# Hybrid pool/HGRN2/RWKV-7 decoder on one core: block-by-block layers against layer 1 first and layer 2 as one pipeline over 32 units

## What is computed

```python
# layer 0 ("layer 1" in this text)
u = h @ ev_w_in                                   # 1024 -> 6 x 512
y_pool = causal_pool_mixer(u[..., :o1], pool_w, pool_scale)      # windows 2, 4, 8, 16
y_hgrn = hgrn2_mixer(u[..., o1:o2], u[..., o2:o3], u[..., o3:o4], lb, hgrn_onorm_g)
out = (concat(y_pool, y_hgrn) * silu(u[..., o4:])) @ ev_w_out
# layer 1 ("layer 2" in this text)
xx = token_shift(h) - h
xm = h[None] + xx[None] * mu[:, None, None, :]    # six mixes: r k v z w a
r, k, v, z = xm[:4] @ w_rkvz
decay = exp(-exp(-softplus(-(w0 + tanh(xm[4] @ w1) @ w2)) - 0.5))
a = sigmoid(a0 + (xm[5] @ a1) @ a2)
# per head of 64, per token: state = state*decay + (state @ -kk) (kk*a)^T + v k^T ; y = state @ r
y = group_norm(y) + bonus
out = (y * silu(z)) @ rw_w_out
```

## Time and profile before

| | us |
|---|---|
| median of 3 runs | 3750.0 (3747.28 to 3751.33) |
| the profiled execution's own time | 3747.55 |
| its span, first to last instruction | 3745.8 |
| PE busy | 3389.4 (90%) |
| DVE busy | 1645.2 (44%) |
| ACT busy | 1264.9 (34%) |
| mean granted TensorE clock | 0.944 of full |

### The profile page before, as it was taken

One profiled execution on the slowest core, in us unless ns is written; L12 is line 12 of the kernel. 1 busy time (PEld: TensorE's weight loads), 2 busy tenths in 40 slices (PEclk: granted clock), 3 DMA queues, 4 the chain that ended last, 5 costly groups with the idle time before them and its releaser, 6 DMA issues.

```text
span 3745.8 us, 76696 instructions
## 1 busy us (share of the span) xinstructions
PE 3389.4 (90%) x33546; PEld 2031.9 (54%) x33546; DVE 1645.2 (44%) x3445; ACT 1264.9 (34%) x2356; POOL 278.4 (7%) x383
## 2 busy tenths in 40 slices
PE   2898799999899869999989887999998987999998
PEld 1554356666356436666646544666654653566663
DVE  7354544443235463444325445444422455444442
ACT  0343233333333323333324332343333333233332
POOL 0010100000011010000000101000000101000000
PEclk8999799999999979999999987999999998899999
DMA  7221211110321121101031211011112211110201
GB/s 315 69 69 68 69 30 43 48 48 30 108 63 55 49 69 48 45 28 48 30 125 46 103 46 47 25 48 48 47 60 83 69 69 46 47 48 25 65 30 51
DMA packets 269508, 230.46 MB, mean 62 GB/s; under 512 B 15548, under 2 KB 251256, under 8 KB 266104
## 3 DMA queue, kind: packets, MB, share of 16 engines
q1 hardware_dynamic: 266872, 217.18, 17.8%
q0 software_dynamic: 2304, 8.39, 0.6%
HBM read 208.76 MB, written 16.78 MB: 60 GB/s over the span
## 4 chain that ended last, share of the span: by engine, by line
PE 81%; DVE 11%; ACT 4%; issue 2%; DMA 1%; SPq 0%; DVEq 0%; ACTq 0%; another core or an unknown queue 0%
PE bank L550 20%; PE bank L424 14%; PE bank L517 8%; PE bank L500 5%; PE bank L649 4%; PE bank L636 4%; PE bank L645 3%; PE bank L457 3%; PE bank L421 3%; DVE xm L1357 2%; PE bank L561 2%; DVE arena L1440 2%; DMA xm<-in_ada_w 1%; PE bank L401 1%; PE bank L692 1%
## 5 line engine op out<-in xcount | busy, mean ns | idle before, releaser
L550 PE MATMUL bank<-xm,wring 128*128 128x512 f32 x2048 | 946.2, 607 | 33.8 <-DVE xm L1357 26.6
L550 PEld LDWEIGHTS bank<-xm,wring 128*128 128x128 f32 x2048 | 381.6, 193 | 504.8 <-issue 445.2
L424 PE MATMUL bank<-arena,wring 128*128 128x512 f32 x1280 | 580.1, 593 | 14.0 <-ACT xm L823 10.2
L424 PEld LDWEIGHTS bank<-arena,wring 128*128 128x128 f32 x1280 | 230.7, 190 | 259.1 <-issue 254.4
L517 PE MATMUL bank<-wring,yT 128*128 128x512 f32 x608 | 281.6, 627 | 30.5 <-DVE yT L1501 20.4
L986 ACT COPY arena<-bank 128x256 f32<-128x256 f32 x256 | 96.6, 377 | 489.1 <-PE bank L649 489.1
L1482 DVE COPY arena<-bank 128x64 f32<-128x64 f32 x256 | 57.6, 225 | 402.4 <-PE bank L682 398.4
L517 PEld LDWEIGHTS bank<-wring,yT 128*128 128x128 f32 x608 | 121.5, 201 | 190.5 <-issue 153.4
L1614 POOL COPY r_Q<-ident 128x512 f32<-128x512 f32 x160 | 98.2, 613 | 1634.5 <-PE bank L649 1626.7
L500 PE MATMUL bank<-wring,yT 128*128 128x512 f32 x416 | 216.4, 626 | 0.0
L649 PE MATMUL bank<-arena,r_Q 64*64 64x32 f32 x5120 | 206.9, 224 | 0.0
(11 more groups left out here) (270 smaller groups left out, 5204.1 us busy)
## 6 DMA issues: line engine op xcount, KB each, us to landing
wring<-in_rw_w_rkvz SPq DMA_DIRECT2D x128, 512.0 KB, 6.3
wring<-in_ev_w_in SPq DMA_DIRECT2D x96, 512.0 KB, 5.2
xm<-in_ada_w SPq DMA_DIRECT2D x16, 1536.0 KB, 11.8
wring<-in_ev_w_out SPq DMA_DIRECT2D x32, 512.0 KB, 7.9
wring<-in_rw_w_out SPq DMA_DIRECT2D x32, 512.0 KB, 4.4
xm<-in_x POOLq DMA_DIRECT2D x16, 512.0 KB, 5.3
arena<-in_x SPq DMA_DIRECT2D x16, 512.0 KB, 5.1
residual_scratch<-arena SPq DMA_DIRECT2D x4, 2048.0 KB, 7.5
```

The lines of the kernel that those rows point to most:

```text
L424: mm = pe.matmul(pj[:, :], w[:, k, :], hT[:, k, 1:1 + TB], start=(k == 0), stop=(k == KC - 1))
L550: mm = pe.matmul(bank[1 if m == PROJ_Z else 0][:, :], w[:, k, :], xmv[MIX_OF[m]][:, k, :], start=(k == 0), stop=(k == KC - 1))
```

## The change

Layer 1 is done for all four blocks first. Each block's input of layer 2 (`h1T`, normed and turned, with one column of the block before) is saved to a DRAM buffer `h1_mem`, its rows to `resid`, tile by tile. The norm of the next block's layer 1 stands inside the output projection of layer 1 (before its last tile group); the layer-2 norm of the block before stands after the first group's projections. The norms scale their rows in place, so a tile is stored before it is scaled.

Layer 2 then runs as one pipeline over 32 units v = 8 b + p. Its input is loaded into slots 4 to 7 of the weight ring (`h_in`), so slots 0 to 3 hold one weight tile each for K, R, V, Z. The mixes of the next block are made inside the periods, in two steps per slice: ACT multiplies by (1 - mu), DVE adds mu times the shifted input: W and A in unit 5 of a block, K, R and V in unit 6, Z in unit 7; `lora_down` ends unit 5's period. The output projection of the block before stands in unit 1, in one piece and without an early part; its residual takes the old rows through one buffer `r_x1`. Only the last block keeps `out_early`.

```diff
@@ sizes and slots
-ARENA = 17184
+ARENA = 19760
-LORA_SLOT = 7
+NB = SEQ // TB
+NU = NB * RP
+LORA_SLOT = 0
+OUT1_ORDER = [2, 0, 1, 3, 4, 5, 6, 7]
+    for v in range(NU):
...
+        for i, m in enumerate("krvz"):
+            uses[i].append((m, v))
+        for i, last in ((0, 2), (1, 2), (2, 1), (3, 1)):
+            if b and p == last:
+                uses[i].append(("o", b - 1))
...
+    for i in range(4, 8):
+        uses[i] += [("h", 0), ("h", 1), ("o", 0), ("h", 2), ("o", 1), ("h", 3), ("o", 2), ("o", 3)]
@@ sync: layer 1
+            group_weights(0, 0)
             for b in range(n_blocks):
+                group_weights(b, 1)
+                if b:
+                    save_input(b - 1)
+                    sp.wait_ge(S["n_tr"], (norm_at(b - 1, 1) + 1) * KC)
                 for j in range(JT):
                     sp.dma_start(xres[:, j, :], x_v[b:b + 1][0][:, j, :]).then_inc(x_in[j], 16)
+                group_weights(b, 2)
+                group_weights(b, 3)
                 for s in range(SLOTS):
+                    load(s, ("o0", b), w_out_v[0][s])
+                if b + 1 < n_blocks:
+                    group_weights(b + 1, 0)
+                for j in range(JT):
+                    sp.wait_ge(S["ob"], b * 8 + 2 * (j + 1))
+                    sp.dma_start(resid[b:b + 1][0][:, j * D:(j + 1) * D], xres[:, j, :]).then_inc(r_save[j], 16)
+            save_input(n_blocks - 1)
@@ sync: layer 2
+            def old_rows(b, j):
+                sp.wait_ge(x_out[j - 1] if j else x_out[JT - 1], 16 * (b + 1 if j else b) + 16)
+                sp.wait_ge(r_save[j], 16 * (b + 1))
+                sp.dma_start(r_x1, resid[b:b + 1][0][:, j * D:(j + 1) * D]).then_inc(S["r_load"], 16)
+            def new_rows(b, j):
+                sp.wait_ge(S["ob"], 8 * n_blocks + 8 * b + 2 * (j + 1))
+                sp.dma_start(out_v[b:b + 1][0][:, j, :], r_x1).then_inc(x_out[j], 16)
...
+            for v in range(-1, NU):
+                b = v // RP - 1
+                if (v + 4) % RP == 0 and v + 4 < NU:
+                    layer_input((v + 4) // RP)
+                if v >= RP and v % RP == 0:
+                    for s in (4, 5, 6, 7, PROJ_V, PROJ_K, PROJ_R):
+                        out_weights(b, s)
+                    gates(v + 3)
+                    out_weights(b, PROJ_Z)
+                    continue
+                if v > RP and v % RP == 1:
+                    for j in range(JT - 1):
+                        old_rows(b, j)
+                        if j < JT - 2:
+                            new_rows(b, j)
+                    weights(v + 1, PROJ_V)
+                    weights(v + 2, PROJ_K)
+                    weights(v + 2, PROJ_R)
+                    weights(v + 1, PROJ_Z)
+                    new_rows(b, JT - 2)
+                    old_rows(b, JT - 1)
+                    new_rows(b, JT - 1)
+                weights(v + 2, PROJ_V)
+                weights(v + 3, PROJ_K)
+                gates(v + 3)
+                weights(v + 3, PROJ_R)
+                weights(v + 2, PROJ_Z)
@@ tensor: out_proj
+                    if l == 0 and gi == len(GROUPS) - 1 and b + 1 < n_blocks:
+                        pe.wait_ge(S["ob"], b * 8 + 4)
+                        norm_transposes(b + 1, 0)
@@ tensor: period
                     turn_values(v)
                     turn_keys(v, 0)
+                    if v > RP and v % RP == 1:
+                        turn_keys(v, 1)
...
+                        pe.wait_ge(S["v_tok"], v + 1)
+                        pe.wait_ge(S["bkt"], v + 1)
+                        pe.wait_ge(S["y_sb"], v)
+                        out_proj(v // RP - 1, 1, early=False)
+                        pe.wait_ge(S["ob"], 8 * n_blocks + 8 * (v // RP - 1) + 2)
                     if inv:
+                        project(v + 1, PROJ_V, 0, 3)
...
+                        project(v + 1, PROJ_V, 3, 5)
+                    if v > RP and v % RP == 1:
+                        pe.wait_ge(S["ob"], 8 * n_blocks + 8 * (v // RP))
...
+                if (v + 3) % RP == 0 and v + 3 < NU:
+                    lora_down((v + 3) // RP)
@@ tensor: the order
+            norm_transposes(0, 0)
+            hgrn_proj(0, 0, 0, NP * KC)
             for b in range(n_blocks):
+                if b:
+                    pe.wait_ge(S["hp_ev"], 1 + (b * HG + 1) * NP)
+                    norm_transposes(b - 1, 1)
                 for g in range(HG):
                     hgrn_mix(b, g)
                 out_proj(b, 0)
+                if b + 1 < n_blocks:
+                    hgrn_proj(b + 1, 0, 0, NP * KC)
+            norm_transposes(n_blocks - 1, 1)
+            lora_down(0)
+            lora_up(0, 0)
+            project(0, PROJ_K, 0, KC)
...
+            for v in range(-1, NU):
+                period(v)
@@ scalar: end of a layer-1 block
+                if b + 1 < n_blocks:
+                    for gi in range(len(GROUPS)):
+                        norm_squares(b + 1, 0, gi)
                 for gi in range(len(GROUPS)):
+                    if gi == len(GROUPS) - 1 and b + 1 < n_blocks:
+                        norm_evac(b + 1, 0)
                     out_squares(b, 0, gi)
                     norm_squares(b, 1, gi)
@@ scalar and vector: mix (ACT's half, then DVE's)
+                    act.mul(xmv[MIX_TO[kind]][:, k, :], h_in[:, k, 1:1 + TB], omu[:, c:c + 1]).then_inc(S["mx_a"], 1)
...
+                    V.wait_ge(S["mx_a"], mix_at(B, kind) + k + 1)
+                    V.scalar_tensor_tensor(out=to, in0=h_in[:, k, 0:TB], scalar=PB[:, c:c + 1], in1=to, op0=ALU.mult, op1=ALU.add)\
+                        .then_inc(S["mx"], 1)
@@ vector: rwkv_period
                 if inv:
+                    rwkv_operands(v + 1)
+                if v > RP and v % RP == 1:
+                    for gi in range(len(GROUPS)):
+                        residual(v // RP - 1, 1, gi)
+                if second_:
+                    mix(B, MIX_K)
+                if third:
+                    mix((v + 1) // RP, MIX_Z)
...
+                    rwkv_masks(v + 1)
+                rwkv_quarter(v, 0)
...
+                    rwkv_scan(v + 2)
+                if second_:
+                    mix(B, MIX_R)
+                rwkv_quarter(v, 1)
...
+                    rwkv_key(v + 2)
+                if first:
+                    mix(B, MIX_W)
+                if second_:
+                    mix(B, MIX_V)
+                rwkv_quarter(v, 2)
...
+                    rwkv_bonus(v + 1)
+                if first:
+                    mix(B, MIX_A)
+                rwkv_quarter(v, 3)
```

More of the change, by code:

```diff
@@ L40, with turn @@
 assert INV_CUT[-1] == INV_PARTS
[L43 to L51, removed]
+BANK0 = [(m, v) for v in range(SEQ // TB * RP) for m in "krv"]
+BANK1 = [x for v in range(SEQ // TB * RP) for x in ([("var", v - 3)] if v >= 3 else []) + [("w", v), ("a", v), ("ks", v)]
+         + ([("z", v - 1)] if v else [])] + [(m, SEQ // TB * RP - i) for m, i in (("var", 3), ("z", 1), ("var", 2))]
+BANKM = [("lo", 0), ("rk", 0)] + [x for v in range(SEQ // TB * RP)
+                                  for x in [("bk", v)] + ([("rk", v + 1)] if v + 1 < SEQ // TB * RP else [])
+                                  + ([("lo", (v + 3) // RP)] if (v + 3) % RP == 0 and v + 3 < SEQ // TB * RP else [])] \
+    + [("var", SEQ // TB * RP - 1)]
+def turn(order, what, v):
+    return order.index((what, v))
 SLOTS = 8
@@ L903, in out_squares @@
                             act.nop().then_inc(w_used[7], 1)
-                        own(act.activation(xm[:, n * 512:(n + 1) * 512], bank[n][:, :], ACT.Square,
+                        if l:
+                            own.wait()
+                        own(act.activation(r_t if l else xm[:, n * 512:(n + 1) * 512], bank[n][:, :], ACT.Square,
                                            accum_out=stat[:, 2, n:n + 1]))
@@ L958, in y_copy, with gate @@
[L958 to L959 removed]
+            def gate(v):
+                act.wait_ge(S["b1_free"], turn(BANK1, "z", v) + 1)
+                act.wait_ge(S["r_arbk"], min(v + 2, NU))
+                act.activation(r_zs, r_z[v % 2], ACT.Sigmoid).then_inc(S["r_sig"], 1)
+            def y_copy(v):
                 act.wait_ge(S["y_ready"], (v + 1) * NCH)
@@ L1100, in _ @@
-                for gi in range(len(GROUPS)):
-                    out_squares(b, 1, gi)
-                own.restart()
+            norm_evac(n_blocks - 1, 1)
+            act.wait_ge(S["h1_save"], n_blocks * 16)
+            for j in range(JT):
+                act.wait_ge(r_save[j], n_blocks * 16)
+            for kind in (MIX_W, MIX_A):
+                mix(0, kind)
+            lora_act(0)
+            mix(0, MIX_K)
+            lora_evac(0, 0)
+            mix(0, MIX_R)
+            project_evac(0, PROJ_K)
@@ new lines, in _ @@
+            key_squares(0)
+            lora_evac(0, 1)
+            mix(0, MIX_V)
+            project_evac(0, PROJ_R)
+            act.wait_ge(S["r_tbm"], 1)
```

(17 more changed lines are left out.)

928 lines of the change are left out of this document (472 added, 456 removed).

## The result

The changed kernel took 3664.7 us in the median of 4 runs (3661.5 to 3672.0), the kernel before 3748.8 beside it: a ratio of 0.978, 95% interval [0.976, 0.980], faster by 84 us. The profiled execution took 3667.7, span 3665.9, mean granted clock 0.951. The forecast was 3650, its range 3595 to 3716.

The account below looks back on a forecast made before the run. PE's work was taken as the floor, only its idle or slow stretches winnable. Each of three boundaries trades 274.2 us for 234.5, -119 in all; +22 once gives a 3648.8 us span, 3650 forecast, range 3595 to 3716.

Parts of the forecast that it names:

- (a): At each block boundary two full periods of 57.4 us replace two short ones: 114.9 us.
- (b): Next block's layer-1 norm inside layer 1's output projection: PE waits for late evacuations, plus low clock, 15.5 us each.
- (c): Previous block's second norm between projections of groups 0 and 1: evacuations paced by ACT, 7 us each.
- (d): SP puts a 2 MB save and four row loads ahead of group 2's weights: 1 us each.
- (e): Six mixes in layer 2's periods: PE waits on late DVE, 20.7 us a block, plus 5 us for the clock.
- (f): LoRA projection at the end of a period: 16 passes for each half, 6.9 us.
- (g): Layer 2's output projection in one piece, with waits before it and on the residual hand-over, plus clock: 63.5 us each.
- switch: Once, from the last layer-1 output projection to the first recurrent unit: 150 us against 129.0, so +21.
- tail: Once, the last rows taken in turns: +1 us.
- One weight slot per matrix: Weight tiles with one slot each cost nothing; rival: loads stall projections in 31 periods, +195 us, 3845, chance 0.05.
- No copy of POOL met a mix: Rival: POOL's identity copies slow DVE's mix slices, one copy in each of 18 bursts, 11 us more, 3661, chance 0.10.
- rival 4: Clock stays low through the small matmuls behind each mix wait: +63 us, 3713, chance 0.16.

Follow-up runs that it names:

- e3: Changed kernel with the layer-1 norm's evacuations moved, on ACT and DVE, ahead of the norm of the tile group before: 3645.4 us, 19.3 less.
- e4: Changed kernel with ACT's products of mixes W and V ahead of its logarithm and exponential instead of behind them: 3641.4 us, 23.3 less.
- e5: Changed kernel with ACT's products of mix Z at the end of unit 6, DVE's slices at the head of unit 7: 3664.2 us, no change.
- e7: Changed kernel with mix Z alone moved behind the scan of unit 7, instead of ahead of the masks: 3651.5 us, 13.2 less.
- e2: Changed kernel with 2 to 7 useless matmuls on constants ahead of PE's waits behind the mixes and the last residual: 3648.7 us, 16.0 less.
- c3: c2 plus three or four matmuls on constants ahead of PE's waits behind mixes A, K, Z and the last residual: 3588.1 us, 22.9 less than c2.
- e1: Changed kernel without the mixes of blocks 1 to 3 on ACT and DVE, signals kept, output different: 3570.1 us, 94.6 less.
- e6: Changed kernel with PE's wait for the last residual in unit 1 taken two slices later: 3649.8 us, 14.9 less.
- c2: Changed kernel with the reorderings of e3, e4 and e6 together: 3611.0 us, 53.7 less.
- c4: c2 with mix Z placed behind the scan of unit 7, as in e7: 3583.6 us, 27.4 less than c2.
- c1: Changed kernel with the reorderings of e3, e4 and e5 together: 3612.6 us, 52 less.

## Why the prediction was right, and where it was off

Term by term, predicted against measured in the changed kernel's span:

| step | predicted | measured | by |
|---|---|---|---|
| (a) ordinary period | 57.4 | 57.5 | stretches |
| (b) layer-1 norm, three | 46.5 | 39.2 (13.7, 14.0, 11.5) | timeline; e3 |
| (c), (d), three | 24 | 20.4 (from one output projection's end to the next one's start 263.5, 263.0, 262.8; before 256.3) | timeline |
| (e) mixes: waits, three | 62.1 | 42.2 | stretches; e4, e5, e7 |
| (e) mixes: clock, three | 15 | 60.4 | stretches; e2, c3 |
| (f) LoRA, each | 6.9 | 7.1 | e1 |
| (g) output projection, each | 63.5 | 65.8 (first block) | stretches; e6 |
| switch | 150 | 143.3 | timeline |
| tail | +1 | +2.3 | end of span |

The differences are -7.3 (b), -3.6 (c, d), -19.9 and +45.4 (e), +6.9 (g), -6.7 (switch) and +1.3 (tail): +16.1 of the 17.1 us.

**Right.** The mechanism: three drains and fills of the pipeline become full periods. (b)'s wait came in the predicted place, the last tile's matmuls at +33.9 where +33.7 was worked out. The term was still too dear, by 7.3 us for the three, for the most part by a flaw in its start: the +20.6 has no low clock in it, while the old projection's 36.3 us hold the 1.8 us behind its first wait, which puts that tile at +22.4. One weight slot per matrix costs nothing. No copy of POOL met a mix.

**The step that failed** is (e), its clock: "For the clock 1 us at each of five (bounds 0 and 3): 5 us" a block. It measured 21.5, 24.7 and 14.2. The rows that it was taken from, a wait of 2.51 us that cost 1.8 more, have large matmuls behind the wait. Behind a mix stand the 64 x 64 and 64 x 32 products of the recurrence, and there the granted clock stayed at the lower of its levels, 1.2 of 2.4 GHz, for 7 to 17 us at a time (first block): unit 6 there has a mean of 0.84, which is 2 x 0.16 x 74 = 24 us at half rate. That the wait brings the low clock is shown by c3 and e2. That the small products are what makes it last is read from the timeline, where it rises only in the next projection; no run changed what stands behind a wait. The right rows were before us: the seventh period, poor in large matmuls, with 0.89. They made rival 4, which had the mechanism and set it at +63; measured, it is +45 over the term. That the forecast still came within 15 us of the median is in good part luck: the clock's 45 us were nearly paid for by waits that were 20 us shorter and by (b), (c), (d) and the switch, 18 us cheaper together. Why the switch was cheaper was not taken apart.

Why the waits were shorter: with DVE's slack as in the earlier trace rows, 5.39 - 1.39 = 4.0 was forecast for K and Z and 2.8 + 0.4 and 3.4 + 0.6 were measured; W and V came at 2.6, not 3.6, A at 1.2 to 1.7, not 4.2, and R, forecast at 1.3, at none. For A no experiment says why; e4 shows that its wait is 3.4 when W's no longer precedes it, so W's wait had taken up a part of A's.

**(g)** was 2.3 us too low at each boundary. The hand-over was forecast at 3.8 and took 6.0, since the store was priced at 2.6 us and took 5.3 beside four weight loads; the wait before the projection was 1.7, not 3.3, and the low clock cost 2.6 (57.5 us busy beyond an ordinary period, for 54.9), not 1.5. That four loads and no other thing made the store slow was read from the timeline and not tried by itself.

## What to carry to other kernels

Price a wait on TensorE with the clock behind it, and look at what runs there: ahead of many small matmuls the granted clock cost here 1.4 times the waits themselves (60 us behind 42), ahead of large ones a wait of 2.5 us cost 1.8 more. So work for another engine that is placed inside a full pipeline belongs where that engine has slack (1 us for eight slices, against 10), and where the stall can't be avoided, matmuls whose result nobody reads can be worth their time, as long as they don't outlast the wait. And before a gain of 5 us is read from one trace, compare the stretches that the edit doesn't touch. Before moving a piece to an earlier place, look for the buffer that it overwrites.

## What the runs showed of the hardware that was not expected

- Filling 3 us waits with matmuls on constants made the kernel faster by 22.9 us (c3 against c2), with the ends of K's and Z's waits unmoved within 0.1 us.
- Units with the same instructions in one kernel differ by 7 us between blocks (unit 6: 66.6 us at 0.95 against 74.0 at 0.84), all of it busy time at the lower clock (59.9 against 67.7). A wait of 0.9 us was followed by a low stretch of some 10 us in two of e7's three units 7, and in none of c4's, whose waits are the same.
- A 512 KB store took 2.6 us alone and 5.3 when it was issued behind four loads of that size on the same queue; the cause was not tried by itself.
- Eight of DVE's two-input slices, 5.39 us alone, took 6.27 where the first of them met POOL's copies, up to 1.09 for one, in the two kernels that place Z so (e5 and c1).
